# MLP of a two-block transformer kernel: norm factor moved from the up product to the down product, fourteen of sixteen up pairs in seven products, last two down quarters in one PSUM bank

## Chip, cores and metric

One core of a Trainium2 chip runs the whole program in one launch. The metric is the device time of that launch in microseconds (us), median of three runs. The profile is one further execution, taken by the hardware profiler.

## The reference, cut to what matters

Two transformer blocks follow each other on one sequence of 512 tokens with 1024 channels, all in fp32. The change touches the MLP that ends the first block, the norms behind it, and how the second block takes them over:

```python
h2 = rmsnorm(x, norm_mlp_g[l])                 # x * rsqrt(mean(x*x) + 1e-6) * g
z = jnp.square(jax.nn.relu(h2 @ w_up[l]))      # 1024 -> 4096
x = x + (z @ w_down[l]).astype(x.dtype)        # 4096 -> 1024
...
x = rmsnorm(x, final_norm_g)                   # end of the first block
...
h = rms_norm(x, norm_mix[l])                   # second block
proj = h @ w_in[l]
q_a, k_a, v_a, u_b, gate_b, gate_c, g_a, g_b = jnp.split(proj, split_points, axis=-1)
```

The rmsnorm has one factor r per token. Since relu and square are positively homogeneous, square(relu(r * y)) is r * r * square(relu(y)): the factor can be left out of the up product and its square applied to the down product, per token.

## The kernel before, in words

**Layout.** Activations are kept channel-major: X is 8 tiles of 128 channels x 512 tokens. Every product is made in three TensorE passes: an operand is split into a rounded part ("hi", a copy on ScalarE, the helper `hi`, L1995) and the rest ("lo", a subtraction on VectorE, the helper `lo`, L2584), and hi*hi, hi*lo and lo*hi are added up in PSUM. Weights are split the same way, in the kernel, after they land in the three raw tiles RAW.

**Units.** `plan` (L120) lists the weight units in the order in which TensorE takes them. A plain unit of the MLP ("up" or "dn") has 8 weight blocks of 128 x 128, so 24 matmuls over 512 tokens (`chunks`, L1528). Two up units can be made together as a pair in seven products (Strassen's scheme, Winograd's form): a pair is seven units "su", each 4 blocks and so 12 matmuls over 256 columns (`seventh`, L1641), with sums of weights made on VectorE (`tile_sum`, L3163) and sums of the activations made once, ahead of the first pair (`h`, `a_hi`, `s13`, `s2`, `s4`, `s_hi`, `s_lo`: ScalarE from L2463, VectorE from L3199). The results of the seven are combined on both engines (`one_out`, `w_less`, `v_less`, `c22`, `c11`, `c12`, `c21`), and relu, square and the split follow. Of the sixteen pairs of the MLP, pairs 4 to 15 are done so; pairs 0 to 3 are eight plain up units.

**Order.** Class `Order` (L235) writes one list of steps; five engine programs (SyncE L1324 with the DMA queue, TensorE L1458, ScalarE L1986, GpSimd L2545, VectorE L2583) walk the same list, each takes its own steps in that order, and semaphores join them. A plain unit is two ticks of the list, an su unit one (`gemm` L448, `seven_up` L687); `later(n, step)` puts a step n+1 ticks on. `take` and `split_to` (L376) place the weight splits ahead of use. The MLP runs (`mlp`, L699): eight up units with the norm behind the first, down quarter 0, pairs 4 to 11, down quarter 1, pairs 12 to 15, down quarters 2 and 3. A quarter is eight dn units, each one PSUM bank that `residual` (L2924, the operation at L2936) adds to X. G has two banks, used in turn.

**Norm of the MLP.** `sq` on ScalarE squares the tiles of X, GpSimd adds seven of them up and VectorE the last (`ADDS`, L114); `acc_hi` and `acc_lo` split the sum, two matmuls with a matrix of ones add over channels, and VectorE and ScalarE make r (L2691, `root` L1998, `refine` L2591). The up units multiply by gain * x without r; `up` on VectorE (L2938) multiplies the PSUM result by r and makes relu and square in one further operation, `up_hi` and `up_lo` split it. The pairs need r earlier: `h` (L3199) makes x * gain * r for all eight tiles, and these are split and summed.

**Behind the MLP.** For each tile of down quarter 3: `residual`, `sq` for c1, `final_a` (the final gain), `sq` for c2, and the split `xsplit` 2. Then `block_b` (L728) begins: the v product (units "vb", four, each 24 matmuls), with `norm2` behind its first unit (two fp32 matmuls with ones, L1774; VectorE L2717), the normed tiles `xn_mul` and `xn_lo` (L2668, L2677), which the first q unit (`qb`) waits for tile by tile, and `cols` (L1781). The first "vb" unit's weights and their followers are split in one step each (`split`).

Of the kernel before, what the change touches and what calls it, by code (L numbers as in the profile page):

```python
# [102 lines left out]
MID, MID_FIRST, MID_PAIRS = 100, 4, 12  # L103
AHEAD_M = 6
RAW_MLP = {("up", 0): (0, 1, 2, 0, 1, 2, 0, 1), ("dn", 0): (2, 0, 1, 2, 0, 2, 0, 1), ("dn", 8): PLACES, ("dn", 16): PLACES,
           ("dn", 24): (2, 0, 1, 2, 0, 1, 2, 0)}
# [7 lines left out]
ADDS = (("mlp", 7), *(("attn", k) for k in range(1, 8)))  # L114
# [5 lines left out]
def plan():  # L120
# [16 lines left out]
    u += up(0) + down(0) + sevens(MID_FIRST, 12) + down(1) + sevens(12, 16) + down(2) + down(3)  # L137
# [39 lines left out]
class Places:  # L177
# [3 lines left out]
    def __init__(self, units):  # L181
# [5 lines left out]
        for v, (name, i, width) in enumerate(units):  # L187
            if name == "su":
# [4 lines left out]
                if units[v + 1][0] != "su":  # L193
                    wide += (half % SLOTS - 4 + 1) // 2
# [27 lines left out]
    def seven_loads(self, v, p):  # L222

        side, key = p % 2, MID + p
        behind = self.pair_held[side]
        sums = ("sums", key, None, max(behind, self.plain_held[3]) if side == 0 else behind)
        self.loads.insert(len(self.loads) - 2 if p == MID_FIRST else len(self.loads), sums)
        self.loads.append(("b22", key, None, max(behind, self.plain_held[2])))
        self.loads.append(("pair", key, side, max(behind, self.plain_held[side])))
        self.count[side] += 1  # L230
        self.pair_nth[key] = self.count[side]
        self.pair_held[side] = v + 7


class Order:  # L235
# [3 lines left out]
    def __init__(self):  # L239
# [11 lines left out]
        self.beside = None  # L251
        self.build()
# [123 lines left out]
    def split_to(self, u, ahead):  # L376
# [7 lines left out]
        while self.split < len(self.units):  # L384
            v = self.split
            if v > u:
                halves += self.units[v][2] // S
                if halves > AHEAD_M + 1 or self.places.free_after[v] >= u:
                    break
            if v > u and self.units[u][0] != "su" and self.units[v][0] != "su" and v >= u + ahead:  # L390
# [242 lines left out]
    def close_a(self):  # L633
# [14 lines left out]
        for n in range(8):  # L648
# [8 lines left out]
            self.put("sq", "mlp", n)  # L657
        self.put("add", "mlp", 7)
# [6 lines left out]
    def down(self, q):  # L665
        for n in range(8):
            self.residual("dn", 8 * q + n, n, ("residual", "dn", 8 * q + n))
            if q == 3:
                self.put("sq", "c1", n)
                self.put("final_a", n)  # L670
                self.put("sq", "c2", n)
                self.put("xsplit", 2, n)

    def prepare_sums(self, section, start):

        for kt in range(4):
            for n, kinds in enumerate((("h",), ("a_hi", "s13"), ("s2", "s4"), ("a_lo", "s_hi"), ("s_lo",))):
                for kind in kinds:
                    self.later(start + 5 * kt + n, kind, section, kt)
# [19 lines left out]
    def mlp(self):  # L699
        self.up(0)  # L700
        self.put("norm", "mlp")
        self.up_out(0)
        self.prepare_sums(0, 1)
        for f in range(1, 8):
            self.up(f)
            self.up_out(f)
        self.down(0)
        for p in range(MID_FIRST, 12):
            self.seven_up(p)
        self.down(1)  # L710
        for p in range(12, 16):
            self.seven_up(p)
        self.down(2)
        self.down(3)
# [13 lines left out]
    def block_b(self):  # L728
        between = {(0, 3): [("norm2",)]}
# [155 lines left out]
    def ffn(self):  # L885
        for f in range(DIRECT):
            if f == 0:
                self.prepare_sums(1, 2)
# [51 lines left out]
def program(nc, a, out):  # L940
# [8 lines left out]
    with ctx:  # L949
# [56 lines left out]
        zbuf = [(MGh, MGl), (XGh, XGl)]  # L1006
# [103 lines left out]
        H = Vh[:, :, :].bitcast(F32)  # L1110
        SVh, SVl = ([QK[:, w, 2 * j:2 * j + 2, :].rearrange("p a (b s) -> p (a b) s", b=2) for j in range(4)] for w in range(2))
        S_AT = 4 + 2 * (1 - DIRECT % 2)
        SUMS = T[:, S_AT:S_AT + 2, :].rearrange("p a (b s) -> p (a b) s", b=2)

        def halves_of(kt):

            return (F[:, 0, :], F[:, 1, :]) if kt % 2 == 0 else (F[:, 2, :], MSK[:, :])
# [18 lines left out]
        SQh, SQl = QK[:, 0, 7, :], QK[:, 1, 7, :]  # L1136
# [7 lines left out]
        NORM = {"attn": (RB[:, :], T[:, 6, :], T[:, 7, :]), "mlp": (RB[:, :], T[:, 2, :], T[:, 3, :]),  # L1144
# [13 lines left out]
        EMPTY = tally("qk", "residual", "up", "qk_b", "conv_g", "conv_y", "branch", "km", "qm", "fg", "fu", "fu_out",  # L1158
# [4 lines left out]
        MOVED = tally("gate", "pool_in", "conv_u", "gate_b")  # L1163
# [62 lines left out]
        z_done, z_hi, z_lo = sem("z_done"), sem("z_hi"), sem("z_lo")  # L1226
# [6 lines left out]
        Z_ACT = tally("relu_a", "relu_b", "square_a", "square_b")  # L1233
# [38 lines left out]
        PREP_ACT, PREP_DVE = tally("s_hi", "a_hi"), tally("h", "s13", "s2", "s4", "s_lo", "a_lo")  # L1272
# [51 lines left out]
        def _(e):  # L1324
            cst = a["cst"]
            for step in steps:
# [5 lines left out]
                elif kind == "load" and places.loads[arg[0]][0] != "unit":  # L1332
# [3 lines left out]
                    if name == "sums" and f == MID + MID_FIRST:  # L1336
                        e.wait_ge(r_done, NRM["norm", "mlp"])
                    elif name == "sums" and f == MID + MID_FIRST + 1:
                        e.wait_ge(prep_dve, PREP_DVE["s_lo", 0, 3])
# [103 lines left out]
                elif kind == "mask_b":  # L1443
                    e.wait_ge(sa_max, 2 * SA["scores_a", 7, 0])
                    e.wait_ge(prep_dve, PREP_DVE["a_lo", 0, 3])
# [12 lines left out]
        def _(e):  # L1458
# [69 lines left out]
            def chunks(u, g, k0, k1):  # L1528

                name, i, width = units[u]  # L1530
                dst = SC[:, 0, :] if g == SPARE else G[:, g % 2, 0:MEM] if name == "km" else G[:, g % 2, :]
                if k0 == 0:
                    if g == SPARE:
# [4 lines left out]
                for k in range(k0, k1):  # L1538
# [6 lines left out]
                    mm(dst, wh, hi, start=(k == 0))  # L1545
# [6 lines left out]
                    t = mm(dst, wl, hi, stop=last)  # L1552
# [29 lines left out]
            left_of = {j: (lambda kt, s=s: (SVh[s][:, kt, :], SVl[s][:, kt, :])) for j, s in ((0, 0), (1, 1), (3, 2), (5, 3))}  # L1582
            left_of[2] = lambda kt: (Vh[:, kt, 0:HALF_S], Vl[:, kt, 0:HALF_S])
            left_of[4] = lambda kt: (Vh[:, 4 + kt, 0:HALF_S], Vl[:, 4 + kt, 0:HALF_S])
# [1828 lines left out]
```

## Time and profile before

| | us |
|---|---|
| median of three runs | 1550.6 (1550.53 to 1551.83) |
| the profiled execution | 1551.22 |
| its span in the trace | 1549.4 |
| TensorE busy in the span | 1538.9 (99%) |
| VectorE, ScalarE, GpSimd busy | 1058.6 (68%), 753.6 (49%), 71.6 (5%) |
| granted TensorE clock | 0.999 of full |

The span begins with the first instruction and ends with the last; the 1.8 us between it and the execution's own time lie around it. Matmul ends are modelled, so a busy TensorE can hide short waits: distances between the starts of matmuls tell more than its busy share. All times of day below are us from the start of the span.

### The profile page before, as it was taken

How to read it: one execution, taken by the hardware profiler on the slowest of the kernel's cores; microseconds unless marked ns; L12 is line 12 of the kernel's file. 1: busy time of each engine (PE TensorE's matmuls, PEld its weight loads, DVE VectorE, ACT ScalarE, POOL GpSimd, SP SyncE). 2: the span in 40 equal slices, each digit the busy share in tenths (PEclk: the TensorE clock that was granted, in tenths of full speed). 3: DMA queues.
4: the chain of work that ended last, by engine and by line, in shares of the span. 5: the costliest groups of instructions: out<-in, count | busy, mean ns of one | idle time of the engine just before them, and what ended most of it. 6: DMA issues, size and time to landing. Idle time of an engine off the chain costs nothing.

```text
span 1549.4 us, 22334 instructions
## 1 busy us (share of the span) xinstructions
PE 1538.9 (99%) x8348; PEld 1331.5 (86%) x8348; DVE 1058.6 (68%) x1759; ACT 753.6 (49%) x1305; POOL 71.6 (5%) x62
## 2 busy tenths in 40 slices
PE   9999999999999999999999999999999999999998
PEld 8888888888799899888888888888888899989987
DVE  6767887768789576357786545455555899948735
ACT  5446677744357445264444334344444545524514
POOL 0000000020000000040000010020002000000002
PEclk9999999999999999999999999999999999999999
DMA  5333223332323222224442232335123333322322
GB/s 193 123 109 97 88 75 96 103 129 86 120 95 110 96 96 100 91 96 122 126 133 65 75 133 86 116 117 161 55 82 109 110 103 109 123 96 82 109 90 75
DMA packets 56235, 161.88 MB, mean 104 GB/s; under 512 B 7232, under 2 KB 8640, under 8 KB 56000
## 3 DMA queue, kind: packets, MB, share of 16 engines
q1 hardware_dynamic: 55504, 159.41, 31.7%
q8 instruction: 67, 1.10, 0.3%
q0 software_dynamic: 320, 0.52, 0.2%
q10 hardware_dynamic: 304, 0.52, 0.1%
q14 instruction: 40, 0.33, 0.1%
HBM read 148.89 MB, written 2.10 MB: 97 GB/s over the span
## 4 chain that ended last, share of the span: by engine, by line
PE 94%; DVE 4%; ACT 1%; issue 1%; DMA 0%; SPq 0%; DVEq 0%; ACTq 0%
PE G L1460 63%; PE TP L1460 11%; PE SC L1460 9%; PE O L1460 5%; PE M L1460 5%; DVE WL L2586 1%; PE TP L1909 1%; PE TP L1855 0%; DVE MGl L2586 0%; DVE T L2944 0%; PE SC L1592 0%; DVE T L2948 0%; DVE QK L2586 0%; DMA T<-QK 0%; PE TP L1958 0%
## 5 line engine op out<-in xcount | busy, mean ns | idle before, releaser
L1460 PE MATMUL G<-XGh,WH 128*128 128x512 f32 x920 | 362.6, 394 | 0.0
L1460 PE MATMUL G<-XGh,WL 128*128 128x512 f32 x920 | 358.8, 390 | 0.0
L1460 PE MATMUL G<-XGl,WH 128*128 128x512 f32 x920 | 358.5, 390 | 0.0
L2586 DVE TENSOR_TENSOR WL<-RAW,WH 128x1024 fp32r<-128x1024 f32 (+2 forms) x269 | 283.0, 1056 | 107.8 <-ACT WH L1996 107.4
L1996 ACT ACTIVATE WH<-RAW 128x1024 fp32r<-128x1024 f32 (+2 forms) x275 | 240.0, 881 | 114.7 <-PE G L1460 81.8
L1460 PEld LDWEIGHTS G<-XGh,WL 128*128 128x128 f32 x920 | 172.8, 188 | 36.5
L1460 PEld LDWEIGHTS G<-XGh,WH 128*128 128x128 f32 x920 | 172.9, 188 | 35.8
L1460 PEld LDWEIGHTS G<-XGl,WH 128*128 128x128 f32 x920 | 173.0, 188 | 34.1
L2936 DVE TENSOR_TENSOR X<-X,G 128x512 f32<-128x512 f32 x75 | 51.5, 686 | 139.5 <-PE G L1460 139.4
L1460 PE MATMUL G<-MGl,WH 128*128 128x512 f32 x372 | 145.0, 390 | 1.1 <-DVE MGl L2586 1.1
L1460 PE MATMUL G<-MGh,WH 128*128 128x512 f32 x372 | 145.1, 390 | 0.0
L1460 PE MATMUL G<-MGh,WL 128*128 128x512 f32 x372 | 144.9, 389 | 0.0
L1460 PEld LDWEIGHTS G<-MGl,WH 128*128 128x128 f32 x372 | 69.9, 188 | 15.8 <-DVE MGl L2586 1.5
L1460 PEld LDWEIGHTS G<-MGh,WL 128*128 128x128 f32 x372 | 69.8, 188 | 14.5
L1460 PEld LDWEIGHTS G<-MGh,WH 128*128 128x128 f32 x372 | 69.9, 188 | 14.4
L2553 POOL TENSOR_TENSOR F<-F 128x512 f32<-128x512 f32 x26 | 34.9, 1340 | 683.9 <-ACT F L2095 683.9
L1996 ACT ACTIVATE MGh<-T 128x512 fp32r<-128x512 f32 x38 | 23.9, 629 | 57.7 <-DVE T L3090 20.9
L1996 ACT ACTIVATE XGh<-X,GN 128x512 fp32r<-128x512 f32 x24 | 17.4, 723 | 63.9 <-DVE X L2936 63.9
L1460 PE MATMUL TP<-QK,WH 128*128 128x256 f32 x248 | 46.0, 283 | 0.0
L1996 ACT ACTIVATE QK<-G 128x512 fp32r<-128x512 f32 (+1 forms) x32 | 17.4, 544 | 54.9 <-PE G L1460 52.6
L1996 ACT ACTIVATE WTh<-RAW 128x512 fp32r<-128x512 f32 (+1 forms) x60 | 35.6, 612 | 13.4 <-DMA RAW<-in_f 12.8
L1996 ACT ACTIVATE WH<-T 128x512 fp32r<-128x512 f32 (+1 forms) x38 | 24.6, 648 | 34.5 <-DVE T L3182 27.7
(426 smaller groups left out, 3279.2 us busy)
## 6 DMA issues: line engine op xcount, KB each, us to landing
RAW<-in_dn SPq DMA_DIRECT2D x30, 512.0 KB, 3.3
RAW<-in_fg SPq DMA_DIRECT2D x22, 512.0 KB, 4.5
RAW<-in_up SPq DMA_DIRECT2D x20, 512.0 KB, 3.4
RAW<-in_g SPq DMA_DIRECT2D x16, 512.0 KB, 3.4
RAW<-in_f SPq DMA_DIRECT2D x14, 512.0 KB, 3.7
X<-in_x SPq DMA_DIRECT2D x16, 256.0 KB, 4.4
RAW<-in_q SPq DMA_DIRECT2D x8, 512.0 KB, 3.3
RAW<-in_k SPq DMA_DIRECT2D x8, 512.0 KB, 3.3
```

The costliest lines, as they stand in the source:

```text
L1460: return e.matmul(dst, st, mv, start=start, stop=stop, skip_group_check=True)
L1909: t = e.transpose(TP[:, c, block], weight_pair(3 * p + g, block)[:, c, :], ID[:, :])
L1996: return e.activation(dst, src, ACT.Copy, scale=scale)
L2553: e.tensor_tensor(acc, acc, sqs[arg[1] % 2], ALU.add).then_inc(acc_done, 1)
L2586: return e.tensor_tensor(dst, src, hi.bitcast(F32), ALU.subtract)
L2936: e.tensor_tensor(X[:, n, :], X[:, n, :], bank, ALU.add).then_inc(g_empty, 1)
```

## The change

The up units are no longer multiplied by r: ScalarE takes relu and square out of PSUM, and `residual` of the down units multiplies the bank by R2 = r * r and then adds (two VectorE operations in place of one). R2 comes from an exponential with power -1 and a refinement of two operations. The sums of activations for the pairs are made from gain * x without r: `hx` on ScalarE makes the two tiles, the split tiles XG serve as four of the seven left operands, and the steps `h`, `a_hi`, `a_lo` of this section go. The norm stands behind the third up unit. Only four plain up units are left, then pairs 2 to 7, down quarter 0, pairs 8 to 11, down quarter 1, pairs 12 to 15, and the last two quarters tile by tile with both in one bank and one `residual` each. At the start of the pairs at most one su unit is split per tick. For the last tile both sums c1 and c2 are finished on VectorE and split, `norm2` takes four matmuls on split operands, and stands behind the first group of the second vb unit. Buffers move accordingly (z of odd quarters to V, `xsplit` 2 to QK).

```diff
-MID, MID_FIRST, MID_PAIRS = 100, 4, 12
+LAST_DOWN = ((0, 2), (1, 2), (0, 3), (1, 3), *((n, q) for n in range(2, 8) for q in (2, 3)))
+STARTS_MID = (0, 5, 7, 9)
+NORM_AT = 2
+MID, MID_FIRST, MID_PAIRS = 100, 2, 14
...
-ADDS = (("mlp", 7), *(("attn", k) for k in range(1, 8)))
+ADDS = (("mlp", 7), ("c1", 7), ("c2", 7), *(("attn", k) for k in range(1, 8)))
...
-    u += up(0) + down(0) + sevens(MID_FIRST, 12) + down(1) + sevens(12, 16) + down(2) + down(3)
+    u += up(0)[0:2 * MID_FIRST] + sevens(MID_FIRST, 8) + down(0) + sevens(8, 12) + down(1) + sevens(12, 16)
+    u += [("dn", 8 * q + n, 1024) for n, q in LAST_DOWN]
...
+                if self.units[v][0] == "su" and self.sevens >= self.clock - self.sevens_from:
+                    break
...
             self.put("xsplit", 1, n)
             self.put("sq", "mlp", n)
+            if n == 4:
+                self.prepare_mid(0)
...
+    def down_both(self):
+        for n, q in LAST_DOWN:
+            step = ("residual", "dn", 24 + n)
+            g = self.bank(step) if q == 2 else self.turn_of[step]
...
+            self.put(*step)
+            self.put("sq", "c1", n)
+            self.put("final_a", n)
+            self.put("sq", "c2", n)
+            if n == 7:
+                for name in ("c1", "c2"):
+                    self.put("add", name, 7)
+                    self.put("acc_hi", name)
+                    self.put("acc_lo", name)
+            self.put("xsplit", 2, n)
...
+    def prepare_mid(self, start):
+        for kt, at in enumerate(STARTS_MID):
+            for n, kinds in enumerate((("hx",), ("s13",), ("s2", "s4", "s_hi"), ("s_lo",))):
+                for kind in kinds:
+                    self.later(start + at + n, kind, 0, kt)
...
         self.put("up", f)
+        self.put("up_sq", f)
         self.later(0, "up_hi", f)
-        self.later(1, "up_lo", f)
+        self.later(1, "up_lo", f, first=True)
...
     def mlp(self):
...
+        for f in range(2 * MID_FIRST):
+            if f == 1:
+                self.sevens_from = self.clock + 1
             self.up(f)
+            if f == NORM_AT:
+                self.put("norm", "mlp")
             self.up_out(f)
...
-        between = {(0, 3): [("norm2",)]}
+        between = {(1, 0): [("norm2",)]}
...
+                elif kind == "up":
...
+                    e.activation(ZP[f % 2], G[:, turn_of[step] % 2, :], ACT.Relu).then_inc(g_moved, 1)
+                elif kind == "up_sq":
...
+                    e.activation(ZP[f % 2], ZP[f % 2], ACT.Square).then_inc(z_act, 1)
...
+                elif kind == "hx":
...
+                    for at, k in zip(halves_of(0, kt), (kt, 4 + kt)):
+                        t = hi(at, X[:, k, :], gain(G_MLP, k))
...
+                        e.tensor_tensor(SCALED_G, bank, R2, ALU.mult).then_inc(g_empty, 1)
+                        e.wait_ge(g_empty, EMPTY[step])
+                        e.tensor_tensor(X[:, n, :], X[:, n, :], SCALED_G, ALU.add).then_inc(dn_added, 1)
...
                 elif kind == "norm2":
                     e.wait_ge(seven_dve, SEVEN_DVE["c12", MID + 15])
-                    e.wait_ge(acc_done, ACC["sq", "c1", 7])
-                    e.matmul(M[:, :], ONEF, STAT["c1"][0], start=True, stop=True).then_inc(sum_done, 1)
...
+                    for name, bank in (("c1", M[:, :]), ("c2", O[:, :])):
...
+                        mm(bank, ONE[:, :], h, start=True)
...
+                        mm(bank, ONE[:, :], l, stop=True).then_inc(sum_done, 1)
```

## Rows read from the trace of the kernel before

**Rows 1.** Page, busy time of each engine: busy us (share of the span) xinstructions

```profile
PE 1538.9 (99%) x8348; PEld 1331.5 (86%) x8348; DVE 1058.6 (68%) x1759; ACT 753.6 (49%) x1305; POOL 71.6 (5%) x62
```

**Rows 2.** Stretch, its us, busy us of PE, PEld, DVE, ACT, POOL; clock; DMA

```profile
372.00:400.00 28.00, 26.94 (x120) 22.00 (x118) 27.31 (x42) 12.87 (x18) 0.00 (x0) 1.00 0.32 106
438.70:519.40 80.70, 80.70 (x674) 80.70 (x673) 72.18 (x132) 56.74 (x110) 0.00 (x0) 1.00 0.32 108
519.40:563.00 43.60, 43.60 (x195) 36.12 (x194) 21.29 (x28) 12.96 (x18) 0.00 (x0) 1.00 0.29 95
```

**Rows 3.** Chain of waits, MLP: start us, us, what

```profile
322.73 32.64 PE G L1460 x144
...
440.23 1.44 PE TP L1460 x12
```

**Rows 4.** Timeline of TensorE, down quarter 0: start, us, operation [idle before <-releaser]

```profile
399.97 0.50 PE L1460 MATMUL G<-MGl,WH 128*128 128x512 f32 x1 [1.06 <-DVE MGl L2586]
```

**Rows 5.** Chain of waits, norm2

```profile
695.79 0.86 PE M L1777 x2
696.65 0.86 PE O L1779 x2
```

**Rows 6.** Timeline of VectorE, first up units

```profile
353.57 0.69 DVE L2586 TENSOR_TENSOR QK<-F,QK 128x512 fp32r<-128x512 f32 x1 [0.70 <-ACT QK L1996]
...
355.93 0.69 DVE L2698 TENSOR_SCALAR T<-M 128x512 f32<-128x512 f32 x1 [0.19 <-PE M L1460]
357.99 0.69 DVE L2595 TENSOR_TENSOR T<-RB 128x512 f32<-128x512 f32 x1 [1.36 <-ACT RB L2004]
...
366.74 0.42 DVE L3215 TENSOR_TENSOR T<-F 128x256 f32<-128x256 f32 x1
...
367.53 0.43 DVE L3221 TENSOR_TENSOR T<-T,F 128x256 f32<-128x256 f32 x1
...
368.33 0.69 DVE L2586 TENSOR_TENSOR MGl<-T,MGh 128x512 fp32r<-128x512 f32 x1
368.93 1.22 DVE L2586 TENSOR_TENSOR WL<-RAW,WH 128x1024 fp32r<-128x1024 f32 x1
370.07 0.69 DVE L2944 TENSOR_TENSOR T<-G,RB 128x512 f32<-128x512 f32 x1
```

**Rows 7.** Timeline of ScalarE, first up units and a pair

```profile
350.76 0.72 ACT L1996 ACTIVATE XGh<-X,GN 128x512 fp32r<-128x512 f32 x1 [3.24 <-DVE X L2936]
351.39 0.62 ACT L2095 ACTIVATE F<-X 128x512 f32<-128x512 f32 x1
...
353.44 1.04 ACT L1996 ACTIVATE WH<-RAW 128x1024 fp32r<-128x1024 f32 x1
...
587.55 0.38 ACT L1996 ACTIVATE F<-SC 128x256 f32<-128x256 f32 x1
```

**Rows 8.** Page, DMA issues: KB each, us to landing

```profile
RAW<-in_up SPq DMA_DIRECT2D x20, 512.0 KB, 3.4
```

**Rows 9.** Timeline of ScalarE, last tile of down quarter 3

```profile
692.07 0.63 ACT L2095 ACTIVATE T<-X 128x512 f32<-128x512 f32 x1 [2.13 <-DVE X L2936]
...
693.35 0.63 ACT L2095 ACTIVATE T<-X 128x512 f32<-128x512 f32 x1
```

**Rows 10.** Timeline of VectorE, from norm2 to the last normed tile

```profile
695.83 1.21 DVE L2586 TENSOR_TENSOR WL<-RAW,WH 128x1024 fp32r<-128x1024 f32 x1
696.96 0.68 DVE L2720 TENSOR_SCALAR T<-M 128x512 f32<-128x512 f32 x1
...
701.87 1.22 DVE L2586 TENSOR_TENSOR WL<-RAW,WH 128x1024 fp32r<-128x1024 f32 x1
703.00 1.41 DVE L2674 SCALAR_TENSOR_TENSOR F<-X,GN,RB 128x512 f32<-128x512 f32 x2
...
717.80 0.68 DVE L2586 TENSOR_TENSOR XGl<-F,XGh 128x512 fp32r<-128x512 f32 x1
```

**Rows 11.** Timeline of TensorE, first q unit, its last tile's second matmul

```profile
719.66 0.39 PE L1460 MATMUL G<-XGl,WH 128*128 128x512 f32 x1
```

More of the change, by code:

```diff
@@ L193, in __init__ @@
                 if units[v + 1][0] != "su":
[L194 removed]
+                    wide += max(half % SLOTS - 4 + 1, 0) // 2
             else:
@@ L225, in seven_loads @@
         behind = self.pair_held[side]
[L226 to L229, printed above, removed]
+        new = [("sums", key, None, max(behind, self.plain_held[3]) if side == 0 else behind),
+               ("b22", key, None, max(behind, self.plain_held[2])),
+               ("pair", key, side, max(behind, self.plain_held[side]))]
+        self.loads += new
         self.count[side] += 1
@@ L699, in mlp @@
     def mlp(self):
[L700 to L704, printed above, removed]
+        for f in range(2 * MID_FIRST):
+            if f == 1:
+                self.sevens_from = self.clock + 1
             self.up(f)
+            if f == NORM_AT:
+                self.put("norm", "mlp")
             self.up_out(f)
[L707 to L714, printed above, removed]
+        for q, (p0, p1) in enumerate(((MID_FIRST, 8), (8, 12), (12, 16))):
+            for p in range(p0, p1):
+                self.seven_up(p)
+            if q < 2:
+                self.down(q)
+        self.down_both()
     def attention_b(self, start):
@@ L1336, in _ @@
                     if name == "sums" and f == MID + MID_FIRST:
-                        e.wait_ge(r_done, NRM["norm", "mlp"])
-                    elif name == "sums" and f == MID + MID_FIRST + 1:
-                        e.wait_ge(prep_dve, PREP_DVE["s_lo", 0, 3])
+                        e.wait_ge(turned, TURN["turn_a", 7, 3])
                     if behind:
@@ L1544, in chunks @@
                         e.wait_ge(*first[0])
-                    mm(dst, wh, hi, start=(k == 0))
+                    mm(dst, wh, hi, start=(k == 0 and not begun))
                     if first:
@@ L1551, in chunks @@
                     last = k == width // P - 1
-                    t = mm(dst, wl, hi, stop=last)
+                    t = mm(dst, wl, hi, stop=(last and not more))
                     if last:
@@ L1687, in _ @@
                         at = slice(kt * P, (kt + 1) * P)
-                        hi, lo = left_of[j](kt)
-                        if first and j in (0, 2):
-                            e.wait_ge(prep_dve, PREP_DVE["s_lo" if j == 0 else "a_lo", 0 if mid else 1, kt])
+                        hi, lo = left_of(j, kt, (XGh, XGl) if mid else (Vh, Vl))
+                        if first and j == 0:
+                            e.wait_ge(prep_dve, PREP_DVE["s_lo", 0 if mid else 1, kt])
+                        elif first and j == 2 and not mid:
+                            e.wait_ge(prep_dve, PREP_DVE["a_lo", 1, kt])
                         mm(bank, wh[:, at], hi, start=(kt == 0 and j < 4))
```

211 lines of the change are left out of this document (135 added, 76 removed).

## The prediction

> **What bounds the kernel now.** First I read the busy times: TensorE works 99% of the span [rows 1], so only two things change the time, what TensorE is given and the waits that the edits make or end. The busy share hides short waits, so next come the pieces of the chain of waits, where distances show: 144 matmuls of 512 columns in 32.64 us, 0.2267 each; twelve of 256 columns in 1.44, 0.120 each [rows 3]. Over all matmuls from 318 us to 740 us I compared each start with these distances. In the MLP one gap stands out: in down quarter 0 the second matmul waits 1.06 for VectorE's z_lo [rows 4]. The third view is busy time by stretch: VectorE works 27.31 of 28.00 in the late up units (why that matmul waits) and 72.18 of 80.70 in the first eight pairs, 9.0 of the 10.08 that a pair takes; in down quarter 1 it has half its time free [rows 2]. So VectorE decides here whether TensorE stalls.
>
> **The change, part by part.**
>
> *Two more pairs.* Four up units go: 4 x 24 x 0.2267 = 21.76. Two pairs come: 2 x 84 x 0.120 = 20.16 [rows 3]. On the path: -1.60.
> The Trainium skill (TensorE: Matmul & The Clock Gate, Back-to-back issue gap) has columns at the full clock plus 2.5 ns, 109 and 216 ns; by that estimate the two pairs would save 2.4 and the sum be 0.8 lower. The rows, 120 and 227, decide.
>
> *Quarter 0 behind six pairs.* Its z is long made, so the 1.06 goes [rows 4]: -1.1. Quarter 3 now starts 10.9 after the last pair (two units of quarter 2), against 43.5; behind the last unit, pair 15 still needs some ten steps of 0.6 to 1.1 on the two engines, about 9 by estimate, so no new wait.
>
> *norm2.* Two fp32 matmuls of 0.86 [rows 5] become four of 0.227: -0.8.
>
> *Down residuals.* 24 get a second operation of 0.60. VectorE has 22 of 43.6 free in a quarter [rows 2], and the bank is free after the first: 0. Without that cover they would cost 0.6 each. One bank for two quarters saves eight additions, on VectorE alone: 0.
>
> *The start of the pairs.* Now the first pair follows 21.8 + 0.45 after the first up unit begins, where 88 lay between. TensorE's own time: up 0 ends at 322.73 + 32.64 = 355.37 [rows 3]; three units and the norm (two matmuls) bring it to 372.1; the fourth block of the first su unit comes nine matmuls on, at 373.2, and needs that block's `s_lo`. What VectorE must do first, in its order from `acc_lo` at 353.57 on [rows 6]: acc_lo 0.60; three blocks s13, s2, s4, 1.59 when in one run (366.74 to 368.33), 4.6; two weight subtractions of 1024 columns at 1.14, 2.3; three s_lo of that size, 3.4; two up_lo, three tile_sum and three su subtractions at 0.60, 4.8: 15.7. The norm stands ahead of the last s_lo: 2.06 from its first operation to the first refinement, during which VectorE waits for ScalarE's Ln and Exp [rows 6], and 1.3 for the two refinements: 3.4. Together 353.57 + 19.1 = 372.7, still in time. But both queues are in order and call on each other. By ScalarE's steps (0.63 for a 512 copy with gain, 0.52 to 0.65 for relu, square and hi, 1.04 for 1024 columns [rows 7]) up_hi 0 ends at 360.0, behind s_hi 1, two hx, relu and square, where VectorE is free at 358.9; the hi of su 0 ends at 364.4, behind s_hi 2 and two hx, where VectorE is free at 363.2; the hi of su 2 costs 0.5 once more; small ones 0.2. That is 3.0: s_lo ends at 375.8, TensorE waits **2.7**. Then nine operations of 0.60 stand before the third pair's second weight sum, on which ScalarE's next hi waits, and `one_out` stands behind that: it ends near 382.4 (587.55 shows 0.38 for one [rows 7]), and TensorE wants it at 375.8 + 0.4 + 4.3 = 380.6: **1.8** more. From there a pair gives VectorE 10.08 for 9.0. Bounds: 0, if all copies find their source ready (the 372.7); 7, if every hand-over costs another 0.1. I take 4.5, the sum's own value.
>
> *Relu and square on ScalarE.* Eight operations of 0.60 leave VectorE; on ScalarE they stand in the chain above, and it has 15 of 28 free [rows 2].
> The Trainium skill (ScalarE: Activation LUTs, Rules for kernel authors) wants relu on VectorE, not ScalarE, which speaks against this. By that rule six of the eight, 3.6, would stand ahead of the last s_lo, and the wait of 2.7 would be 6.3; the trace disagrees here, since VectorE is the engine that TensorE waits for.
>
> *Behind the MLP.* The last dn unit ends one vb unit (5.44) before norm2, near 690.35 [rows 5]. Now VectorE multiplies and adds (1.4), ScalarE squares for c1 at 691.8 and for c2 1.28 later [rows 9], and then the sums of both go in turn to VectorE (add), ScalarE (acc_hi), VectorE (acc_lo), at 0.6 to 0.7 a step: acc_lo of c2 ends near 696.9, the split of X's last tile at 697.5. norm2 comes at 697.0 on TensorE: it just fits. But two weight subtractions of the vb units now stand before norm2's VectorE steps, where one stood before (695.83) and one behind (701.87) [rows 10]: they end near 700.1. The steps from 696.96 to 701.87 are 4.9, so `xn_mul` starts at 705.1 and not 703.0, 2.1 later. In the trace the last xn_lo ends at 718.48 [rows 10], TensorE needs it at 719.66 [rows 11]: 1.2 spare, and it now comes 0.8 sooner. New wait in the first q unit: 2.1 - 1.2 + 0.8 = **1.7**. Bounds: 0, if those subtractions fall into the pauses of the sums; 2.7, if the sums run one hand-over (1.0) later. I take 1.7; the order of the list is fixed, so they cannot move up.
>
> *Queues and DMA.* The raw tiles of the first pair are asked for once up 2 is split (357.0). With 3.4 to landing [rows 8] they are there at 360.4 to 361; the first tile_sum wants them at 361.5: 0, with half a microsecond of cover.
>
> **Sum.** -1.6 - 1.1 - 0.8 + 2.7 + 1.8 + 1.7 = +2.7. On the profiled execution, 1551.2 (span 1549.4 and 1.8 around it), that gives 1553.9; this run lies 0.6 above the median of the runs shown, so against the median, 1550.6, **1553.3**.
>
> **Rivals.**
> (A) The two engines stay in step: VectorE ends the fourth block by 373.2 and the q unit's tiles come in time. Then only the gains are left, -3.5: 1547.1. For it: VectorE's bare work ends at 372.7. Against: it needs all 3.0 of hand-over waits gone.
> (B) One of the two places stalls, not both: 1549 to 1552.
> (C) Slower: the first pair's raw tile lands late. Four loads leave SP's queue together at 357.0; if the pair's waits behind the others, it lands at 363.8 (two landings in a row), 2.3 after the first tile_sum wants it; that holds all of VectorE behind it, and the wait at the fourth block grows by as much: 1555.6. It decides from a landing later than 361.5. For it: half a microsecond of cover. Against: one load of twice a half's size takes 3.4, and the queues overlap.
> That the change does less TensorE work than it says is excluded by the counts.
>
> **How the numbers follow.** A measurement of this kernel can tell 0.2%, 3.1 us, from no change. Forecast 0.45 (its own range 1551.3 to 1555.3: same 0.26, slower 0.19); A 0.25 (with remnants of a wait: faster 0.15, same 0.10); B 0.15 (same); C 0.15 (slower). Faster 0.15, same 0.51, slower 0.34. The range takes in A and C: 1547.0 to 1556.0.
>
> **What would show it.** In the timeline of TensorE: su units beginning near 372, an idle of 2 to 3 before a matmul on a QK operand in the first one, released by VectorE's s_lo, and one of 1 to 2 at the fifth unit, released by ScalarE; no idle at quarter 0; matmuls of 0.227 in norm2; an idle of 1.5 to 2 in the first q unit, released by XGl. The forecast is wrong if VectorE is not waiting for ScalarE between 359 and 371, or if the landing of the first pair's tile ends one of its waits.

## The result, and the profile after

The changed kernel takes 1556.72 us (median of seven runs, 1555.95 to 1559.5), the kernel before 1551.83 in the runs beside it: a ratio of 1.0035, 95% interval 1.0025 to 1.0045, or 5.4 us (3.9 to 7.0) slower. The forecast was 1553.3, 2.7 above its own base, with 1547.0 to 1556.0 as its range. The direction was right, the size was not, and the result lies outside the range. The profiled execution of the changed kernel took 1557.71 (span 1555.9).

The busy line of the page answers to [rows 1]; TensorE is 99% busy as before, and the line shows nothing of the loss:

```profile
PE 1539.3 (99%) x8420; PEld 1335.4 (86%) x8420; DVE 1064.5 (68%) x1774; ACT 770.1 (49%) x1337; POOL 69.0 (4%) x60
```

Profiled executions differ by up to 3.6 us already ahead of the changed part, so I measure a **stage** in each: from a PV product that both kernels have (it waits 0.4 us for VectorE's X) to the first G product behind a set of transposes in attention B, where the tails are alike again (797.1 us to the end of the span in both). Timeline of TensorE, the kernel before, then after:

```profile
303.75 0.50 PE L1460 MATMUL O<-WTh,Vh 128*128 128x512 f32 x1 [0.44 <-DVE X L2896]
...
752.30 0.47 PE L1460 MATMUL G<-XGh,WH 128*128 128x512 f32 x1
```

```profile
304.32 0.50 PE L1506 MATMUL O<-WTh,Vh 128*128 128x512 f32 x1 [0.45 <-DVE X L2996]
...
378.25 0.80 PE L1506 MATMUL O<-QK,WTh 128*128 128x256 f32 x2 [4.37 <-DVE QK L2676]
...
440.98 0.40 PE L1506 MATMUL G<-MGl,WH 128*128 128x512 f32 x1
...
702.33 0.39 PE L1506 MATMUL M<-XGh,ONE 128*128 128x512 f32 x1
...
726.07 0.50 PE L1506 MATMUL G<-XGl,WH 128*128 128x512 f32 x1 [1.77 <-DVE XGl L2676]
...
758.84 0.47 PE L1506 MATMUL G<-XGh,WH 128*128 128x512 f32 x1
```

The stage is 448.55 before and 454.52 after: 5.97 more, which is the whole loss. Its landmarks: the fourth block of the first su unit waits 4.37 for VectorE's last `s_lo`; quarter 0's second matmul waits for nothing (1.06 in [rows 4]); norm2's four matmuls are ordinary ones of 512 columns (two of 0.86 in [rows 5]); the first q unit waits 1.77 for the last normed tile ([rows 11] shows no wait).

What follows the first wait stands in the chain of waits (start, us, what), the answer to the second line of [rows 3], and in the busy time by stretch (columns as in [rows 2]):

```profile
378.25 1.01 PE O L1506 x3
379.26 2.56 PE TP L1506 x12
381.82 2.56 PE SC L1506 x12
384.38 1.51 PE TP L1506 x12
```

```profile
373.70:378.30 4.60, 0.23 (x3) 0.05 (x1) 3.13 (x5) 3.96 (x8) 0.00 (x0) 0.93 0.00 0
378.30:384.40 6.10, 6.10 (x29) 6.10 (x30) 5.91 (x10) 4.22 (x8) 0.00 (x0) 0.50 0.04 11
384.40:436.30 51.90, 51.89 (x432) 51.68 (x431) 48.28 (x88) 39.62 (x76) 0.00 (x0) 1.00 0.35 118
```

TensorE stood still, and behind the standstill its granted clock is 0.50, the lower of its two levels (1.2 against 2.4 GHz): two whole units take 2.56 instead of 1.44. The wait that the prediction put at the fifth unit is not there; the slow units took its place. At the end of the table the pairs run without a gap.

VectorE's timeline answers to [rows 6] and [rows 10]:

```profile
352.19 0.67 DVE L3045 TENSOR_TENSOR X<-X,G 128x512 f32<-128x512 f32 x1
...
355.71 0.69 DVE L2676 TENSOR_TENSOR Vl<-F,Vh 128x512 fp32r<-128x512 f32 x1 [0.70 <-ACT Vh L2055]
...
363.62 0.69 DVE L3281 TENSOR_TENSOR T<-RAW,T 128x512 f32<-128x512 f32 x1
...
375.64 0.69 DVE L2695 SCALAR_TENSOR_TENSOR T<-T,RB 128x512 f32<-128x512 f32 x1 [1.43 <-ACT RB L2063]
...
376.98 1.22 DVE L2676 TENSOR_TENSOR QK<-T,QK 128x1024 fp32r<-128x1024 f32 x1
...
703.20 2.36 DVE L2676 TENSOR_TENSOR WL<-RAW,WH 128x1024 fp32r<-128x1024 f32 x2 [0.20 <-ACT WH L2055]
705.48 0.68 DVE L2820 TENSOR_SCALAR T<-M 128x512 f32<-128x512 f32 x1
...
725.33 0.68 DVE L2676 TENSOR_TENSOR XGl<-F,XGh 128x512 fp32r<-128x512 f32 x1
```

`acc_lo` is at 355.71, against 353.57 in [rows 6]: 2.14 later, of which 0.57 lies ahead of the stage, so 1.57 is the change's. The last `s_lo` starts at 376.98 and holds TensorE. The lower rows are the q unit's case: two weight splits in one run stand ahead of norm2's first step, and the last tile's low part comes at 725.33.

### The profile page after: what moved, and what is told of

Read it like the earlier page. It is cut to its first block, busy times and chain, and to the rows that moved or that the text cites. A ratio compares the mean times of both kernels' runs of the same rounds, so it can differ in the third digit from the quotient of the medians.

```text
span 1555.9 us, 22585 instructions
## 1 busy us (share of the span) xinstructions
PE 1539.3 (99%) x8420; PEld 1335.4 (86%) x8420; DVE 1064.5 (68%) x1774; ACT 770.1 (49%) x1337; POOL 69.0 (4%) x60
## 4 chain that ended last, share of the span: by engine, by line
PE 91%; DVE 4%; ACT 2%; issue 1%; DMA 1%; SPq 0%; DVEq 0%; ACTq 0%
PE G L1506 61%; PE TP L1506 10%; PE SC L1506 9%; PE O L1506 5%; PE M L1506 5%; DVE WL L2676 1%; ACT WH L2055 1%; PE TP L1968 1%; PE TP L1914 0%; DMA RAW<-in_va 0%; DVE F L2772 0%; DMA T<-QK 0%; DVE X L3045 0%; DVE XGl L2676 0%; DVE QK L2676 0%
## 5 line engine op out<-in xcount | busy, mean ns | idle before, releaser
L1506 PE MATMUL G<-XGh,WH 128*128 128x512 f32 x760 | 300.1, 395 | 0.0
L1506 PE MATMUL G<-XGl,WH 128*128 128x512 f32 x760 | 296.1, 390 | 1.8 <-DVE XGl L2676 1.8
L1506 PE MATMUL G<-XGh,WL 128*128 128x512 f32 x760 | 296.2, 390 | 0.0
L1506 PEld LDWEIGHTS G<-XGl,WH 128*128 128x128 f32 x760 | 142.9, 188 | 30.3 <-DVE XGl L2676 2.2
L1506 PEld LDWEIGHTS G<-XGh,WL 128*128 128x128 f32 x760 | 142.6, 188 | 30.3
L1506 PEld LDWEIGHTS G<-XGh,WH 128*128 128x128 f32 x760 | 142.7, 188 | 29.8 <-ACT MSK L2332 0.2
L3045 DVE TENSOR_TENSOR X<-X,G 128x512 f32<-128x512 f32 x43 | 29.5, 686 | 73.4 <-PE G L1506 73.3
L1506 PE MATMUL G<-Vh,WH 128*128 128x512 f32 x160 | 62.3, 389 | 0.0
L1506 PE MATMUL G<-Vl,WH 128*128 128x512 f32 x160 | 62.3, 389 | 0.0
L1506 PE MATMUL G<-Vh,WL 128*128 128x512 f32 x160 | 62.2, 389 | 0.0
```

Of the source, the lines that this page charges most:

```text
L1506: return e.matmul(dst, st, mv, start=start, stop=stop, skip_group_check=True)
L3045: e.tensor_tensor(X[:, n, :], X[:, n, :], bank, ALU.add).then_inc(g_empty, 1)
```

## The experiments

All are edits of the changed kernel, built to tell three things apart: which chain sets the start of the pairs, what the low clock costs, and what sets the q unit. "Fifth unit" is the start of the first pair's fifth su unit, counted from the PV product at the head of the stage; waits and stage are of the profiled execution; the ratio is to the kernel before.

| kernel | wait, 4th block | fifth unit (its wait) | wait, q unit | stage | ratio |
|---|---|---|---|---|---|
| changed | 4.37 | 81.41 (none) | 1.77 | 454.52 | 1.0035 [1.0025, 1.0045] |
| 1 norm's end later | 1.50 | 80.10 (4.06) | 1.77 | 455.66 | 1.0047 [1.0033, 1.0061] |
| 2 filler products | 1.63 | 80.36 (1.47) | 1.79 | 455.21 | 1.0029 [1.0018, 1.0041] |
| 3 norm2 in turn | 4.33 | 80.38 (0.23) | 0.54 | 452.40 | 1.0024 [1.0016, 1.0033] |
| 4 six units | none | 86.31 (none) | 1.78 | 450.79 | 1.0007 [0.9998, 1.0016] |
| 5 sums on GpSimd | 7.59 | 84.77 (none) | 1.77 | 457.88 | 1.0058 [1.0045, 1.0072] |
| 6 relu on VectorE | 4.71 | 82.70 (1.74) | 1.76 | 455.93 | 1.0048 [1.0035, 1.0060] |
| 7 six, norm2, relu | none | 90.54 (2.12) | 0.51 | 452.12 | 1.0027 [1.0016, 1.0038] |
| 8 GpSimd, norm2 | 7.58 | 84.50 (none) | 0.51 | 456.36 | 1.0050 [1.0037, 1.0063] |
| 9 six, norm2 | none | 86.57 (none) | 0.52 | 448.16 | 0.9993 [0.9985, 1.0002] |
| 10 eight, norm2 | none | 96.29 (none) | 0.51 | 447.78 | 0.9995 [0.9986, 1.0004] |
| 11 shorter s_lo | 2.30 | 79.01 (0.71) | 1.76 | 452.21 | 1.0024 [1.0015, 1.0033] |
| 12 six, norm later | none | 89.13 (2.50) | 0.51 | 452.19 | 1.0018 [1.0009, 1.0027] |

Against the changed kernel, the ratios of 4, 5, 9 and 10 differ by more than the intervals leave open, and so do those of 7 and 12 against 9. The ratios of 1, 2, 3, 6, 7, 8 and 11 do not differ clearly from the changed kernel's; what is said of these rests on the waits and the stage, of one profiled execution each.

**1. The norm's last two steps behind the last s_lo.**

```diff
                 self.put("norm", "mlp")
+                self.later(0, "norm_end")
...
-                    if arg[0] == "mlp":
-                        refine_square(ms, r, tmp)
-                    elif arg[0] != "mq":
+                    if arg[0] not in ("mlp", "mq"):
                         refine(ms, r, tmp)
+                elif kind == "norm_end":
+                    r, ms, tmp = NORM["mlp"]
+                    refine_square(ms, r, tmp)
```

> One edit to the changed kernel: on VectorE, the two closing steps of the MLP norm (which wait 1.43 us for ScalarE's exponential) come right behind the last s_lo instead of ahead of it. Nothing is left out. Theory (the s_lo chain on VectorE holds TensorE, and the 4.4 us wait pulls the granted clock down): the last s_lo starts 2.8 us earlier, TensorE's wait at the fourth block falls from 4.5 to about 1.8 us, the granted clock stays at 1.00 as it did around the 1.8 us wait of the q unit, and the units behind take 1.44 us and not 2.56. That is 5.4 us, of which the first pair's fifth and sixth units give back up to 2.8 (they run into one_out and v_less, which VectorE reaches only about 384): 1.5 to 4 us faster than the changed kernel, 2.5 as the single value. Rival 1 (VectorE's work up to the first pair's results sets the end, wherever TensorE waits): only the 1.43 us of VectorE's idle time is saved, 1.4 us faster. Rival 2 (late loads of the first pair): no change.

Not faster: the stage is 1.1 longer, and the ratio lies 1.9 us higher, with intervals that overlap. The theory, in the form I had it, falls. TensorE's timeline and then ScalarE's ahead of the second wait:

```profile
377.43 0.50 PE L1507 MATMUL O<-QK,WTh 128*128 128x256 f32 x2 [1.50 <-DVE QK L2677]
386.43 0.58 PE L1507 MATMUL SC<-XGh,WH 128*128 128x256 f32 x1 [4.06 <-ACT F L2056]
```

```profile
385.47 0.63 ACT L2056 ACTIVATE WH<-F 128x512 fp32r<-128x512 f32 x1 [0.57 <-DVE F L3291]
386.01 0.37 ACT L2056 ACTIVATE F<-SC 128x256 f32<-128x256 f32 x1
```

The wait fell to 1.50 as expected, but 4.06 came back at the fifth unit, for `one_out`. That unit began 1.31 earlier than in the changed kernel, near rival 1's figure. `one_out` (386.01) stands in ScalarE's queue behind a weight's high part, and that waits for a block sum of the next pair, which VectorE reaches late. And behind the wait of 4.06 the clock fell instead, which cost more than the 1.31.

**2. Twelve products ahead of the wait.**

```diff
+                        if first and j == 0 and mid and kt == 3:
+                            e.wait_ge(sa_max, 2 * SA["scores_a", 7, 3])
+                            for _ in range(12):
+                                mm(SC[:, 1, :], ONE[:, :], XGh[:, 0, :], start=True, stop=True)
                         if first and j == 0:
                             e.wait_ge(prep_dve, PREP_DVE["s_lo", 0 if mid else 1, kt])
```

> One edit to the changed kernel: 12 products of 512 columns (2.7 us) into a bank that is free, put on TensorE ahead of its wait for the last s_lo. Their sums are overwritten and used by nothing. Theory (the clock falls because TensorE stands still there): the remaining wait is about 1.8 us, the granted clock stays at 1.00, the first pair's units take 1.44 us, and of the 2.6 us of slow units about 0.7 comes back as a wait for v_less at the sixth unit: about 1.9 us faster. Rival (the units of 2.56 us wait for something and the clock is only a sign of it): no change, the units stay at 2.56. Rival 2 (the clock falls whatever TensorE does there, since many engines start together): granted clock 0.50 as before, no change.

```profile
373.44 2.91 PE L1506 MATMUL SC<-XGh,ONE 128*128 128x512 f32 x12
...
377.98 0.51 PE L1506 MATMUL O<-QK,WTh 128*128 128x256 f32 x2 [1.63 <-DVE QK L2680]
...
384.39 0.39 PE L1506 MATMUL SC<-XGh,WH 128*128 128x256 f32 x1 [1.47 <-ACT F L2059]
...
724.86 0.50 PE L1506 MATMUL G<-XGl,WH 128*128 128x512 f32 x1 [1.79 <-DVE XGl L2680]
...
725.45 0.63 PE L1506 MATMUL G<-XGh,WH 128*128 128x512 f32 x1
725.88 0.63 PE L1506 MATMUL G<-XGl,WH 128*128 128x512 f32 x1
```

With TensorE at work for most of the wait the clock stays at 1.00 and units take 1.44: both rivals fall, the long standstill is what lowers the clock. But 1.47 comes back at the fifth unit, so the slow units cost only 1.05 net (81.41 against 80.36), not 2.6. The ratios of the two kernels can't be told apart, and this profile has a loss of its own: behind the q unit's wait of 1.79 the clock fell here (matmuls of 512 columns start 0.43 apart, eight of them, 1.5 us), where after the same wait in the changed kernel's profile it did not.

**3. norm2's sums in turn, norm2 earlier.**

```diff
-                for name in ("c1", "c2"):
-                    self.put("add", name, 7)
-                    self.put("acc_hi", name)
-                    self.put("acc_lo", name)
+                for kind in ("add", "acc_hi", "acc_lo"):
+                    for name in ("c1", "c2"):
+                        self.put(kind, *((name, 7) if kind == "add" else (name,)))
...
-        between = {(1, 0): [("norm2",)]}
+        between = {(0, 3): [("norm2",)]}
...
```

> One edit to the changed kernel: the last additions, high parts and low parts of the two sums of squares are issued in turn (both sums at once) and norm2 is issued four products of the first V unit earlier, so that its VectorE steps stand ahead of the second of the two weight splits. Nothing is left out. Theory (norm2's VectorE steps queue behind two weight splits of 1.2 us each, and the q unit waits for what follows): the q unit's wait falls from 1.8 to about 0.7 us, 1.1 us faster. Rival (the q unit waits for its weights or for ScalarE's part of the last normalised tile, with norm2 off its path): no change.

```profile
722.34 0.50 PE L1505 MATMUL G<-XGl,WH 128*128 128x512 f32 x1 [0.54 <-DVE XGl L2675]
```

The q unit's wait is 1.23 shorter, as the theory has it; the ratio is 1.7 us lower, which alone would not be clear. The stage lost 2.1: in this execution the clock came back one unit sooner behind the first wait (fifth unit at 80.38).

**4. Six plain units.**

```diff
-MID, MID_FIRST, MID_PAIRS = 100, 2, 14
+MID, MID_FIRST, MID_PAIRS = 100, 3, 13
...
-RAW_MLP = {("up", 0): (0, 1, 2, 1), ("dn", 0): PLACES, ("dn", 8): PLACES, ("dn", 16): (0, 3, 0, 0, 2, 1, 0, 2),
+RAW_MLP = {("up", 0): (0, 1, 2, 0, 2, 0), ("dn", 0): PLACES, ("dn", 8): PLACES, ("dn", 16): (0, 3, 0, 0, 2, 1, 0, 2),
```

> The changed kernel with six plain up units and 13 pairs in seven products, instead of four and 14 (half of that part of the change undone). Nothing is left out. Theory: TensorE has 10.9 us more of plain work ahead of the first pair and VectorE some 4 us more of its own, so that the wait for the last s_lo, the low clock behind it and the waits of the first pair's results all go (7.1 us together); one pair less costs 0.8: about 6.3 us faster than the changed kernel, near 1550.4. Rival 1 (each added pair costs of itself, by VectorE's load in the pairs): half of the change's loss, 2.7 us faster. Rival 2 (the loss is outside the pairs): 0.8 us slower.

```profile
373.76 0.50 PE L1506 MATMUL G<-XGh,WH 128*128 128x512 f32 x1 [0.28 <-ACT F L2332]
380.03 0.50 PE L1506 MATMUL G<-XGh,WH 128*128 128x512 f32 x1 [0.52 <-ACT MSK L2332]
```

4.3 us less by the ratios (1553.3): the waits of the pairs' start are gone with one pair less. From the fifth unit to its end the stage is 8.6 shorter, a pair's 10.1 less the 1.5 of low clock named below, so the pairs themselves cost no more than TensorE's own time. That excludes both rivals; the ratio alone would leave the first one's 2.7 open. It stops 2 to 3 short of the forecast: two new waits for ScalarE's relu (0.44 and 0.67 from matmul to matmul), and in this profile too the clock fell behind the q unit's 1.78.

**5. Block sums on GpSimd.**

```diff
+        ON_POOL = [step for step in steps if step[0] == "tile_sum" and step[1] in first_pairs[0]]
...
         @block.gpsimd
...
+                elif step in POOLED:
+                    tile_sum(e, *arg)
```

> One edit to the changed kernel: the eight sums of weight blocks of the first two pairs are made by GpSimd, which is idle there, instead of VectorE; six of them stood in VectorE's queue ahead of the first pair's results. Nothing is left out. Theory, as the runs so far leave it (one chain of VectorE and ScalarE steps, from the wo phase to one_out, sets when the first pair's fifth unit starts: 80.1 to 80.4 us after the last PV product in three runs that waited at three different places, 81.6 where the halved clock came on top): three sums less ahead of the last s_lo and six less ahead of one_out, 0.6 us each: the wait at the fourth block falls from 4.5 to about 2.7 us, the fifth unit starts at about 78 instead of 81.6, 3 us faster than the changed kernel (1.5 to 4.5). Rival 1 (ScalarE's own steps set one_out): the fifth unit stays at 80, 0 to 1.5 us faster. Rival 2 (GpSimd's additions of 1.3 us each, four in a chain, come too late for ScalarE's high parts): slower by 1 us or more.

VectorE's timeline, then GpSimd's:

```profile
363.82 1.22 DVE L2725 TENSOR_TENSOR WL<-RAW,WH 128x1024 fp32r<-128x1024 f32 x1
...
368.09 2.32 DVE L2725 TENSOR_TENSOR QK<-T,QK 128x1024 fp32r<-128x1024 f32 x1
370.51 1.33 DVE L3332 TENSOR_TENSOR T<-T 128x256 f32<-128x256 f32 x1
371.77 1.50 DVE L3333 TENSOR_TENSOR T<-T 128x256 f32<-128x256 f32 x1
...
377.14 0.68 DVE L2845 TENSOR_SCALAR T<-M 128x512 f32<-128x512 f32 x1
```

```profile
364.13 2.07 POOL L1373 TENSOR_TENSOR T<-RAW,T 128x512 f32<-128x512 f32 x1 [12.75 <-DMA RAW<-in_up]
...
369.41 2.15 POOL L1388 TENSOR_TENSOR F<-F,RAW 128x512 f32<-128x512 f32 x1
371.52 1.47 POOL L1373 TENSOR_TENSOR T<-RAW,T 128x512 f32<-128x512 f32 x1
...
376.75 1.59 POOL L1383 TENSOR_TENSOR T<-T,RAW 128x512 f32<-128x512 f32 x1
```

3.6 us slower by the ratios; neither the theory's gain nor the second rival's reason (ScalarE's first high part waits 0.1 to 0.2 for GpSimd's sum, the others do not). While GpSimd adds, VectorE's operations with two operands in SBUF last 2.32 instead of 1.22 and 1.33 to 1.50 instead of 0.42; the one that reads a PSUM bank (377.14) keeps its 0.68, and the one of 1024 columns that began 0.31 ahead of an addition (363.82) keeps its 1.22, while that addition takes 2.07. VectorE lost more than the three sums it gave away, and the last `s_lo` came later (7.59). The Trainium skill (SBUF — State Buffer, Who interferes with whom) says that a VectorE instruction with two SBUF inputs contends with a GpSimd instruction that reads SBUF; these rows agree.

**6. Relu on VectorE.**

```diff
-                    e.activation(ZP[f % 2], G[:, turn_of[step] % 2, :], ACT.Relu).then_inc(g_moved, 1)
...
+                    e.tensor_scalar(ZP[f % 2], G[:, turn_of[step] % 2, :], 0.0, None, ALU.max).then_inc(g_empty, 1)
```

> One edit to the changed kernel: the relu of the four plain up units is a VectorE step (maximum with zero, out of the bank) and no longer ScalarE's; the square stays on ScalarE. Nothing is left out. Theory (VectorE is the later of the two in the chain to one_out): four more steps of 0.6 us on it, partly covered by the 4.7 us in which it waits for ScalarE there: 1 us slower, between 1 faster and 2.4 slower. [...]

1.4 us slower by the stage (2.0 by the ratios, whose intervals overlap): the first wait is longer (4.71), and the fifth unit waits 1.74 where it waited for nothing. That is within the theory's bounds (1 faster to 2.4 slower). A gain, as there would be if ScalarE were the later of the two engines, is not there. The rule of the Trainium skill (ScalarE: Activation LUTs, Rules for kernel authors), relu on VectorE and not ScalarE, does not pay in this stage; that fits VectorE being the later of the two engines, and experiments 7 and 9, which differ by this edit alone, show it clear of the noise.

**7. Six units, norm2 in turn, relu on VectorE.** The edits of 3, 4 and 6.

> Three edits to the changed kernel: six plain up units and 13 pairs (run before: 3.4 us faster), the two sums of norm2 in turn and norm2 four products earlier (run before: 1.7 us faster), and the relu of the six plain units on VectorE. Nothing is left out. Theory: the waits of 0.44 and 0.67 us of the plain units on ScalarE, seen with six of them, go; the q unit's wait of 1.8 us falls to 0.7, and so does the low clock that followed it in that run (1.5 us): 1.1 + 1.2 + up to 1.5 less than 1553.3, near 1550.3 (1549.5 to 1551.5). Rival (VectorE becomes late with the relu, and holds the first pair): 1551.5 to 1554.

```profile
381.51 0.50 PE L1505 MATMUL G<-XGh,WH 128*128 128x512 f32 x1 [2.02 <-DVE MSK L2801]
```

The rival, and more of it: 1555.8. Relu on VectorE makes the plain units wait longer (2.02 for it here, 0.87 at the same place in 9), and holds the pair as well (2.12 at the fifth unit, none in 9).

**8. Sums on GpSimd and norm2 in turn.** The edits of 3 and 5.

> The two edits together on the changed kernel: the first two pairs' block sums on GpSimd, and the two sums of norm2 in turn with norm2 four products earlier. Nothing is left out. Theory: they stand in places that don't touch, so the gains add: 3 and 1.7 us off the changed kernel, near 1552.0 (1550.5 to 1553.5). Rival (the sums on GpSimd bring nothing): as with norm2 alone, 1.7 us off.

The forecast of 1552.0 is missed, at 1559.2. The two edits do add up, but GpSimd's is a loss: the stage is 1.5 shorter than in 5, of which the q unit's wait is 1.26, as norm2 in turn gives.

**9 and 10. Six or eight units, norm2 in turn, relu left on ScalarE.** The edits of 3 and 4; for eight, `MID_FIRST, MID_PAIRS` are 4 and 12 and the plain units' raw tiles (0, 1, 2, 0, 1, 2, 0, 1).

> Two edits to the changed kernel: six plain up units and 13 pairs, and the two sums of norm2 in turn with norm2 four products earlier; relu stays on ScalarE. Nothing is left out. Theory: no long wait is left anywhere, so the granted clock falls nowhere; 1.2 us of the q unit's wait and the low clock that followed it in the profiled run of the six-unit kernel go: 1551.0 (1550.2 to 1552.0), at or just under the kernel before. Rival (the two edits meet somewhere): 1552.5 to 1553.5, as with six units alone.

> As the run with six plain units and norm2 in turn, but with eight plain up units and 12 pairs, as many as the kernel before has; of the change the plain units without the norm, the order of the pairs and the down quarters, and norm2 in high and low parts stay. Nothing is left out. Theory (with six units the start of the pairs no longer holds TensorE): one pair less is 0.8 us more than with six, and two more plain units wait up to 0.7 us each for ScalarE: 1552.3 (1551.5 to 1553.5). Rival (the pairs' start still costs with six, somewhere the gaps don't show): the same time as with six or less.

Medians 1551.16 and 1551.0, the kernel before 1552.11 beside them. The longest wait of TensorE inside the six-unit kernel's stage, and its clock there and at the q unit, which waits 0.52:

```profile
380.20 0.50 PE L1505 MATMUL G<-XGh,WH 128*128 128x512 f32 x1 [0.87 <-ACT MSK L2331]
```

```profile
366.00:390.00 24.00, 22.89 (x117) 19.03 (x116) 19.62 (x31) 18.76 (x32) 0.00 (x0) 1.00 0.41 134
716.00:725.00 9.00, 8.48 (x37) 6.69 (x37) 7.99 (x13) 6.48 (x10) 0.00 (x0) 1.00 0.37 116
```

The clock stays at 1.00 and the theory's figure for six units holds. Eight units were forecast 1.3 slower than six and are not: the pair less costs 0.8 and the second wait for relu (0.87) goes in exchange. Both stand at the kernel before or a shade under; the intervals reach just over 1.

**11. Shorter low parts.**

```diff
-                    lo(sums_to(1, kt), sums_of(section), sums_to(0, kt)).then_inc(prep_dve, 1)
+                    few = slice(0, 8 if section == 0 and kt >= 2 else HALF_S)
+                    lo(sums_to(1, kt)[:, :, few], sums_of(section)[:, :, few], sums_to(0, kt)[:, :, few]).then_inc(prep_dve, 1)
```

> One edit to the changed kernel: the low parts of the last two s sums (s_lo 2 and s_lo 3) are made for 8 of 256 columns each; the other columns of these low parts hold what was there, so that the output is not the reference's. VectorE has some 1.0 us less work at each of the two, in its queue ahead of TensorE's wait and of one_out; ScalarE has the same work. Theory (VectorE's queue sets the start of the pairs): the wait at the fourth block falls from 4.5 to about 2.5 us, the granted clock stays at 1.00, the fifth unit starts at 78.4 instead of 81.6 us after the last PV product: 3.2 us faster than the changed kernel (2 to 4). Rival 1 (ScalarE's steps and splits set one_out): the wait at the fourth block falls too, but one_out stays at 80.4: 1.2 us faster, the clock's part alone. Rival 2 (the loads of the first pair set it): no more than 1.2 us faster, and VectorE waits for a transfer ahead of the pair's block sums.

```profile
376.78 0.61 PE L1506 MATMUL O<-QK,WTh 128*128 128x256 f32 x2 [2.30 <-DVE QK L2676]
...
383.93 0.38 PE L1506 MATMUL SC<-XGh,WH 128*128 128x256 f32 x1 [0.71 <-ACT F L2055]
```

The first wait fell by 2.07, and the fifth unit waits for `one_out` until 79.01 where three kernels waited for it until 80.1 to 80.4: 1.1 to 1.4 of the 2.1 that VectorE was spared reach `one_out`, so rival 1's unmoved `one_out` falls. For the rest VectorE now waits on ScalarE: 0.21 and 0.35 ahead of two up_lo, where it waited for nothing in the changed kernel. So VectorE's queue leads and ScalarE follows close behind. 2.3 us by the stage and 1.7 by the ratios (not clear of the noise), for the theory's 3.2: the clock fell behind 2.30 as well (units of 2.56), and the fifth unit came 0.6 later than forecast.

**12. Six units, the norm behind the fifth.** As 9, with `NORM_AT = 4`.

> The run with six plain units and norm2 in turn, and one edit more: the MLP norm stands behind the fifth plain unit instead of the third. Nothing is left out. With the norm behind the third unit, TensorE waited 0.40 us at the fifth plain unit and 1.03 us at the sixth for ScalarE's relu; the norm's two ScalarE steps (1.2 us) and its VectorE steps (3.4 us with the wait between them) stood ahead of these. Theory (the chain of VectorE and ScalarE up to the first pair has slack with six units, so that the norm is free behind the fifth): both waits go, 1.4 us faster than that run, near 1549.8. Rival (the norm then holds the relu of the fifth unit or the first pair's one_out): no gain, 1551 to 1552.5.

```profile
375.57 0.69 DVE L3282 TENSOR_TENSOR T<-RAW,T 128x512 f32<-128x512 f32 x1 [3.56 <-DMA RAW<-in_up]
```

Worse than 9 by 4 us: without the norm in its way VectorE comes to the first block sum 3.56 us ahead of the pair's raw tile, everything behind it is held, and the norm then stands ahead of `one_out` (a wait of 2.50, and a low clock behind it). With the norm in its old place, in 9, it waited 0.26 there: with six units the load is as late as VectorE, and the norm had been filling that wait.

## Why the prediction was wrong

Right, by the steps of the prediction: the pairs themselves run at 1.44 a unit (two more pairs, -1.6); quarter 0's wait is gone (-1.1); norm2 is at 0.227 a matmul (-0.8); the down residuals' second operation and the shared bank cost nothing. **Behind the MLP** was right in its mechanism and nearly in size: `xn_mul` behind two weight splits, 1.77 waited (1.93 lost) for a forecast of 1.7, and experiment 3 takes 1.2 of it away by moving norm2's steps ahead of the second split.

The hand-overs between the two engines, forecast at 3.0, were 2.6: from `acc_lo` to the last `s_lo` VectorE waited 1.00, 1.14 and 0.44 for ScalarE, beside the norm. Two slips in the prediction's sums (three times 1.59 is 4.8, not 4.6; from 373.2 to 375.8 is 2.6, not 2.7) change nothing in what follows.

**The failing step is "The start of the pairs"**, forecast at 2.7 + 1.8 = 4.5. The first four su units would end at 74.1 on the stage's clock without any wait (68.32 + 4 x 1.44); the fifth began at 81.41: 7.3 lost. Two terms are missing.

- *The entry of the chain, 1.6.* I started VectorE's list at `acc_lo`, at the time that the old trace gave it, and counted the three blocks behind. The first block is prepared ahead of `acc_lo`, in the wo phase: three s steps of 1.59 together and an `s_lo` of 1.2, and I costed them at nothing, with no cover named. VectorE had some pause there, as the row of before shows (it waited 0.97 for TensorE):

```profile
350.04 0.69 DVE L2936 TENSOR_TENSOR X<-X,G 128x512 f32<-128x512 f32 x1 [0.97 <-PE G L1460]
```

  After, the same residual stands at 352.19 with no idle, and `acc_lo` is 1.57 late. Counted from the head of the stage, VectorE's two timelines agree to 0.03 us up to a weight's low part, before and then after, with ScalarE and GpSimd after:

```profile
336.67 1.52 DVE L2586 TENSOR_TENSOR WL<-RAW,WH 128x1024 fp32r<-128x1024 f32 x1 [0.72 <-ACT WH L1996]
```

```profile
338.47 1.23 DVE L2676 TENSOR_TENSOR WL<-RAW,WH 128x1024 fp32r<-128x1024 f32 x1 [1.95 <-ACT WH L2055]
...
342.42 1.51 DVE L3324 TENSOR_TENSOR T<-T 128x256 f32<-128x256 f32 x1
```

```profile
336.16 1.32 ACT L2055 ACTIVATE T<-X,GN 128x512 f32<-128x512 f32 x2
...
342.32 1.34 POOL L2643 TENSOR_TENSOR F<-F 128x512 f32<-128x512 f32 x1 [4.65 <-ACT F L2154]
```

  There ScalarE's first `hx` (1.32) stands ahead of the weight's high part, and VectorE comes 1.23 late. Then `s2` lasts 1.51 and not 0.42, beside GpSimd's addition of squares: the stretch that experiment 5 made worse is in the changed kernel already. By an estimate from these rows it makes up some 1.1 of the 1.57, since `s_hi`, `s_lo` and the next residual follow on it, and the residuals behind it no longer wait for TensorE. No run moved this first block, so the entry is read from the two traces and not tested.

  From there on the working holds: 22.2 us forecast from `acc_lo` to the end of the last `s_lo`, 22.5 measured (355.71 to 378.2). `one_out` was forecast to end at 382.4, 78.7 on the stage's clock; it released the fifth unit at 80.1 to 80.4 in experiments 1, 2 and 3, which is that 1.6.
- *The clock, about 1.0 to 1.3.* The forecast priced a wait at its length. Behind 4.37 the clock was 0.50 for 6 us; TensorE reached the fifth unit at 81.41 instead of 80.1 to 80.4. The slow units hid what would have been the second wait, so their 2.6 us count for half or less.

With them: 4.5 + 1.6 + 1.2 = 7.3, and the sum is 2.7 + 2.8 + 0.2 (q unit) + 0.2 (a short wait of the pair ahead of quarter 0) = 5.9, the stage's 5.97.

On the rivals. (A) and (B) did not come. (C) did not decide the changed kernel, but its premise was nearer than I gave it. SP's queue in the changed kernel's timeline:

```profile
359.62 0.38 SPq L1394 DMA_DIRECT2D RAW<-in_up  x1
```

The pair's tile was asked for at 359.62, not 357.0, since the loads stand behind a split (up 2's) that is itself in VectorE's late queue (its low part ends at 359.1). By the same trace it landed 3.9 us later, at 363.5, just ahead of VectorE's sum at 363.62. Of the half microsecond of cover 0.1 was there, by luck; only VectorE's own lateness hid it. In experiment 12 it decides.

## What to carry to other kernels

When work moves ahead of a chain, follow it back to where the moved work begins, and cost its first piece too, also where it lands in a phase that looked idle. Where two engines with in-order queues hand results to each other, a wait that is taken away at one consumer comes back at the next (experiments 1 and 2): what helps is less work on the leading queue (experiment 11, by the stage), or more independent work for the waiting engine (experiments 4, 9, 10). And a wait of TensorE of some microseconds is priced with the slow matmuls behind it, less what they hide.

## What the runs showed of the hardware

TensorE's granted clock, by the profiles: behind waits of 1.06 (before), 1.27, 1.47, 1.50, 1.63, 1.74, 2.02 and 2.12 us it stayed at 1.00; behind 2.30, 2.50, 4.06, 4.33, 4.37, 4.71, 7.58 and 7.59 it fell to 0.50, for some 3 to 6 us (one to two su units); behind the q unit's 1.76 to 1.79 it fell in two profiles of seven (experiments 2 and 4, 1.5 us each) and stayed in the others. What decides it no run shows. The mean clock of the changed kernel's seven runs was 0.995 to 0.997, that of the kernel of experiment 9 and of the kernel before 0.998 to 0.999 in the runs beside each other, so the low clock is not the profiled execution's alone. In experiment 11 the mean clock lay between 0.996 and 0.999, so a fall need not come in every run.

GpSimd's additions of 128x512 stretch VectorE's operations on two SBUF operands that begin beside them by a factor of 1.9 to 3.6 (in the rows shown), and take 1.27 to 2.15 themselves. The one operation shown that began first kept its 1.22.
